# Hybrid encoder layer on one core: own PSUM banks for the up rows of even and odd tiles, earlier down additions, and silu as a sigmoid on ScalarE with a multiply on GpSimd during the attention

## What is computed

```python
h = x @ w_in                      # columns for three mixers
pool_out = multiscale_pool(h[..., :COL_Z], pool_w) * pool_scale
ssd_out = ssd_mixer(z, xbc, dt)   # silu(causal conv of width 4), chunked scan, gate silu(z), RMS norm
sb_out = stick_breaking_attention(q, k, v)      # 6 heads of 64, strictly causal, 128-query blocks
x = layer_norm(ALPHA * x + concat(pool_out, ssd_out, sb_out) @ w_out, ln1_g, ln1_b)
up = causal_depthwise_conv(x @ w_up, conv_w, conv_b)      # width 3, 2 x 2816 columns
ffn = (silu(up[..., :D_FF]) * up[..., D_FF:]) @ w_down
ple = sigmoid(x @ ple_w_gate) * (p @ ple_w_proj)
x = layer_norm(ALPHA * x + ffn + ple, ln2_g, ln2_b)
```

## Time and profile before

| | us |
|---|---|
| median of 3 runs | 1437.26 |
| lowest, highest | 1435.45, 1437.79 |
| the profiled execution | 1435.54 |
| its span in the trace | 1433.8 |

### The profile page before, as it was taken

One profiled execution on the slowest core, in us unless ns is written; L12 is line 12 of the kernel. 1 busy time (PEld: TensorE's weight loads), 2 busy tenths in 40 slices (PEclk: granted clock), 3 DMA queues, 4 the chain that ended last, 5 costly groups with the idle time before them and its releaser, 6 DMA issues.

```text
span 1433.8 us, 16333 instructions
## 1 busy us (share of the span) xinstructions
PE 1320.9 (92%) x6084; PEld 1057.1 (74%) x6084; DVE 879.5 (61%) x1060; ACT 507.4 (35%) x747; POOL 208.1 (15%) x141
## 2 busy tenths in 40 slices
PE   7999999899767999999999999999999999999993
PEld 5787788677655788788877777777777777777772
DVE  3536646534387845532467676767676776767778
ACT  4445445444544224312333232423232332323412
POOL 0000000000271000510012111111122021111116
PEclk9999999899988999999999999999999999999996
DMA  5101000000001311310020111102010101111102
GB/s 217 52 23 45 30 30 30 30 30 15 1 1 59 103 44 60 102 45 30 30 74 30 60 44 44 59 31 83 32 59 29 59 29 59 44 45 59 59 16 117
DMA packets 22947, 71.93 MB, mean 50 GB/s; under 512 B 2544, under 2 KB 2800, under 8 KB 22896
## 3 DMA queue, kind: packets, MB, share of 16 engines
q1 hardware_dynamic: 22896, 71.22, 14.6%
HBM read 67.02 MB, written 4.19 MB: 50 GB/s over the span
## 4 chain that ended last, share of the span: by engine, by line
PE 59%; DVE 18%; ACT 5%; issue 5%; DMA 1%; ACTq 1%; POOL 1%; DVEq 0%; SPq 0%; POOLq 0%
PE ps L667 12%; PE ps L669 12%; PE ps L668 12%; PE ps L1009 5%; PE ps L1011 5%; PE ps L1010 5%; DVE conv_ff L1764 4%; DVE conv_ff L1767 2%; PE ps L761 2%; ACT conv_ff L1343 2%; DVE w_lo L553 1%; PE ps L721 1%; PE ps L745 1%; PE ps L804 1%; ACT w_hi L548 1%
## 5 line engine op out<-in xcount | busy, mean ns | idle before, releaser
L1816 DVE TENSOR_TENSOR acc<-acc,ps 128x512 f32<-128x512 f32 x176 | 117.6, 685 | 71.2 <-PE ps L669 71.2
L667 PE MATMUL ps<-x_hi,w_hi 128*128 128x512 f32 x336 | 142.0, 423 | 14.1 <-DVE x_lo L502 10.5
L667 PE MATMUL ps<-h_hi,w_hi 128*128 128x512 f32 x320 | 127.6, 399 | 11.3 <-DVE acc L1816 11.3
L668 PE MATMUL ps<-x_lo,w_hi 128*128 128x512 f32 x336 | 134.6, 400 | 0.0
L669 PE MATMUL ps<-x_hi,w_lo 128*128 128x512 f32 x336 | 134.2, 399 | 0.0
L669 PE MATMUL ps<-h_hi,w_lo 128*128 128x512 f32 x320 | 126.6, 396 | 0.0
L668 PE MATMUL ps<-h_lo,w_hi 128*128 128x512 f32 x320 | 126.6, 396 | 0.0
L1009 PE MATMUL ps<-mix_hi,w_hi 128*128 128x512 f32 x320 | 126.6, 396 | 0.0
L1010 PE MATMUL ps<-mix_lo,w_hi 128*128 128x512 f32 x320 | 126.6, 396 | 0.0
L1011 PE MATMUL ps<-mix_hi,w_lo 128*128 128x512 f32 x320 | 126.6, 396 | 0.0
L1009 PE MATMUL ps<-t_hi,w_hi 128*128 128x512 f32 x240 | 96.8, 403 | 18.2 <-DVE conv_ff L1767 18.2
(11 more groups left out here) (240 smaller groups left out, 2847.9 us busy)
## 6 DMA issues: line engine op xcount, KB each, us to landing
raw<-u_up SPq DMA_DIRECT2D x44, 512.0 KB, 3.3
raw<-u_in SPq DMA_DIRECT2D x22, 512.0 KB, 3.3
down_raw<-u_down SPq DMA_DIRECT2D x44, 256.0 KB, 2.8
x_stage<-u_x SPq DMA_DIRECT2D x8, 512.0 KB, 7.7
raw<-u_out SPq DMA_DIRECT2D x8, 512.0 KB, 3.2
x_nat<-x_nat SPq DMA_DIRECT2D x8, 512.0 KB, 3.3
raw<-u_gate SPq DMA_DIRECT2D x8, 512.0 KB, 3.3
out<-o_norm SPq DMA_DIRECT2D x8, 512.0 KB, 2.6
```

The costliest lines, as they stand in the source:

```text
L667: mm(dst, w_hi, x_hi, start=first, stop=False)
L668: mm(dst, w_hi, x_lo, start=False, stop=False)
L1816: v.tensor_tensor(dst, dst, ps[:, bank, :], ALU.add).then_inc(dn_added, 1)
```

## The change

It has three parts.

1. In the feed-forward Y becomes banks 0, 1 for even pairs and 6, 7 for odd ones. The waits of PE follow: S2 of the even pair waits for the value row of the even pair before (`row_done` + 2 instead of + 4), S2 of the odd pair has no wait of its own except in the last chunk, and the first down product waits for all rows of the chunk before, where the third waited for three of them. In the last chunk the down products use banks 4, 5, 0, 1, and the final transposes pairs 1 and 3 instead of 0 and 1.
2. In DVE's order of a chunk the taps of the even gate row and the first five down additions come ahead of the split of A11 of the odd pair.
3. The ten silus become a sigmoid (ACT) and a multiply (GpSimd) at ticks of the attention: for the seven conv tiles at `GATE_AT`, the tick after the last tap (ticks 23, 29, 36, 53, 59, 66 and 73), for z0 to z2 at ticks 75, 77 and 80. Conv j waits for multiply j - 1 instead of for conv j - 1, at the earliest three ticks after the last tap: conv 6 moves from tick 66 to tick 68 and its taps from 68, 69, 70 to 69, 70, 72. The exp/ln table is loaded right after the barrier.

```diff
...
+GATE_LAG = 3
 CONV_AT, TAPS_AT = [], []
 for _name in H_TILES[:7]:
-    CONV_AT.append(max([evacuated_at(("tile", _name)) + 1] + [t[-1] + 1 for t in TAPS_AT[-1:]]))
+    CONV_AT.append(max([evacuated_at(("tile", _name)) + 1] + [t[-1] + GATE_LAG for t in TAPS_AT[-1:]]))
     TAPS_AT.append([s for s in range(CONV_AT[-1] + 1, NTICK) if s not in SPLIT_AT][:CONV - 1])
+GATE_AT = [t[-1] + 1 for t in TAPS_AT]
+for _name in H_TILES[7:10]:
+    GATE_AT.append(max(evacuated_at(("tile", _name)) + 1, GATE_AT[-1] + 2))
 DT_AT = evacuated_at(("turn", 3)) + 1
 SUMS_AT = 2 + next(s for s, d in enumerate(DONE_AT) if any(it[0] == "sums" for it in d))
...
             + [(d, k) for k in range(2) for d in (D0A, D1A, D0B, D1B)])
 PRODUCTS = {A11: 1, S1: 2, S2: 3, S3: 4, A12: 5, S4: 6, A22: 7}
 LASTC = CHUNKS - 1
-X_BANK, Y_BANK = (4, 2), 0
-DOWN_BANKS = (6, 7, 2, 3)
+X_BANK, Y_BANK = (4, 2), (0, 6)
+DOWN_BANKS, LAST_BANKS = (6, 7, 2, 3), (4, 5, 0, 1)
 def ops(c):
...
     dt_v = sem("dt_v")
     dt_a = sem("dt_a")
-    tap_done, conv_done, silu_done = sem("tap_done"), sem("conv_done"), sem("silu_done")
+    tap_done, conv_done, gate_done, silu_done = sem("tap_done"), sem("conv_done"), sem("gate_done"), sem("silu_done")
     d_full = sem("d_full")
     d_free = [sem("d_free%d" % i) for i in range(4)]
     decay_done = sem("decay_done")
...
     def up_row(pp, r):
-        b = Y_BANK if r else X_BANK[pp]
+        b = (Y_BANK if r else X_BANK)[pp]
         return ps[:, b:b + 2, :].rearrange("p b n -> p (b n)")
     def per_head(row, c):
...
             elif t == 2:
                 eng.wait_ge(u_free, 2 * KT)
             elif t == 3:
-                eng.wait_ge(row_done, 2)
                 column_tile(dst, slot, n, (1,)).then_inc(n1_read, 1)
             column_tile(dst, slot, n, (0,) if t == 3 else (0, 1)).then_inc(u_full, 1)
         def product(c, o, pp, it=0):
             first, second = slice(0, HALF), slice(HALF, S)
-            x, y = X_BANK[pp], Y_BANK
+            x, y = X_BANK[pp], Y_BANK[pp]
             bank, t_h, t_l = {
                 A11: (x, mh[:, 0:4, first], ml[:, 0:4, first]), S1: (x + 1, t1h, t1l), S2: (y + 1, t2h, t2l),
                 S3: (y, mh[:, 0:4, second], ml[:, 0:4, second]), A12: (x, mh[:, 4:8, first], ml[:, 4:8, first]),
...
             first = 16 * (c - 1 + pp)
             if k >= 4 or pp:
                 eng.wait_ge(dn_added, first + k - 3 + 16 * it)
-            bank = 4 + k % 4 if c == LASTC else DOWN_BANKS[k % 4]
+            bank = (LAST_BANKS if c == LASTC else DOWN_BANKS)[k % 4]
             h_h, h_l = (h2h, h2l) if pp else (hh, hl)
             for i in range(2):
                 o = ((D0A, D1A), (D0B, D1B))[j // 4][i]
...
             eng.wait_ge(row_done, 4 * (c - 1) + 1 + 4 * it)
             product(c, A11, 0, it)
             product(c, S1, 0, it)
-            eng.wait_ge(row_done, 4 * (c - 1) + 4 + 4 * it)
+            eng.wait_ge(row_done, 4 * (c - 1) + 2 + 4 * it)
             if c == 1:
                 eng.wait_ge(t_lo, 12)
             product(c, S2, 0, it)
...
             if c < LASTC:
                 eng.wait_ge(dn_added, 16 * (c - 1) + 16 + 16 * it)
             product(c, S1, 1, it)
-            eng.wait_ge(row_done, 4 * c + 2 + 4 * it)
+            if c == LASTC:
+                eng.wait_ge(row_done, 4 * (c - 1) + 4)
             product(c, S2, 1, it)
             product(c, S3, 1, it)
             eng.wait_ge(p1_done, 2 * (c - 1) + 2 + 2 * it)
...
             even(c, it)
             for k in range(16):
-                if k == 2:
-                    eng.wait_ge(row_done, 4 * (c - 1) + 3 + 4 * it)
+                if k == 0:
+                    eng.wait_ge(row_done, 4 * (c - 1) + 4 + 4 * it)
                 down(c, k, 0, it)
             even_last(c, it)
             odd(c, it)
...
             elif m >= 2:
                 eng.wait_ge(o_nrm, m - 1)
             for kt in range(KT):
-                last = turn(two(m % 2)[:, kt * P:(kt + 1) * P], acc[:, kt, m * P:(m + 1) * P])
+                last = turn(two((1, 3)[m % 2])[:, kt * P:(kt + 1) * P], acc[:, kt, m * P:(m + 1) * P])
             last.then_inc(o_full, 1)
         for t in range(4):
...
         even(LASTC)
         even_last(LASTC)
         odd(LASTC)
-        eng.wait_ge(row_done, 4 * LASTC + 1)
+        eng.wait_ge(row_done, 4 * LASTC + 2)
         for k in range(16):
             down(LASTC, k, 0)
         for k in range(16):
...
                 for hh_ in range(2):
                     wait_evacuated(eng, PLACE[(H_TILES[j], hh_)])
                 if j:
-                    eng.wait_ge(conv_done, j)
+                    eng.wait_ge(silu_done, j)
                 act(cv[:, j, :], ht[:, j, :], ACT.Identity, scale=param("conv_w", 4 * j + 3),
                     bias=param("conv_b", j)).then_inc(tap_done, 1)
+            if n in GATE_AT:
+                j = GATE_AT.index(n)
+                if j < 7:
+                    eng.wait_ge(conv_done, j + 1)
+                    act(ht[:, j, :], cv[:, j, :], ACT.Sigmoid).then_inc(gate_done, 1)
+                else:
+                    for hh_ in range(2):
+                        wait_evacuated(eng, PLACE[(H_TILES[j], hh_)])
+                    eng.wait_ge(silu_done, j)
+                    act(ht[:, 6, :], ht[:, j, :], ACT.Sigmoid).then_inc(gate_done, 1)
             if n == DT_AT + 1:
                 eng.wait_ge(dt_v, 1)
                 act(sm[:, 2, :], sm[:, 1, :], ACT.Exp).then_inc(dt_a, 1)
...
                 eng.wait_ge(decay_done, 1)
                 act(sm[:, 8, :], sm[:, 8, :], ACT.Exp).then_inc(dt_a, 1)
                 act(sm[:, 9, :], sm[:, 7, :], ACT.Exp).then_inc(dt_a, 1)
-            if n == NTICK + LAG - 1:
-                eng.wait_ge(conv_done, 7)
-                for j in range(3):
-                    act(cv[:, j, :], cv[:, j, :], ACT.Silu).then_inc(silu_done, 1)
         meet(eng, 1)
...
             pair = task_place(name)[0]
             return two(pair), d_free[pair]
-        for j in (3, 4):
-            act(cv[:, j, :], cv[:, j, :], ACT.Silu).then_inc(silu_done, 1)
+        nc.scalar.preload_act_table_set("natural_log_exp_and_others")
         for g in range(2):
             src, free = task("bt%d" % g)
             act(bn[:, g, :, :].rearrange("p m n -> p (m n)"), src, ACT.Copy).then_inc(free, 1)
-        for j in (5, 6):
-            act(cv[:, j, :], cv[:, j, :], ACT.Silu).then_inc(silu_done, 1)
-        for j in range(3):
-            act(ht[:, 7 + j, :], ht[:, 7 + j, :], ACT.Silu).then_inc(silu_done, 1)
         for g in range(2):
             src, free = task("cb%d" % g)
             act(cb[:, g, :], src, ACT.Copy).then_inc(free, 1)
...
             eng.wait_ge(hg_done, i + 1)
             act(cv[:, 3 + i, :], cv[:, i, :], ACT.Square).then_inc(sq_done, 1)
-        nc.scalar.preload_act_table_set("natural_log_exp_and_others")
         def pool_mean(i):
             eng.wait_ge(pool_sum, i + 1)
...
             eng.wait_ge(o_aff, m + 1)
             if m >= 4:
                 eng.wait_ge(stored[m % 4], 16 * (m // 4))
-            act(on[:, m % 4, :], two(m % 2), ACT.Identity, scale=st[:, m, 13:14],
+            act(on[:, m % 4, :], two((1, 3)[m % 2]), ACT.Identity, scale=st[:, m, 13:14],
                 bias=st[:, m, 12:13]).then_inc(o_nrm, 1)
...
         def combine(c, pp, step, it=0):
             n = 10 * (c - 1) + 5 * pp
-            x, y = X_BANK[pp], Y_BANK
+            x, y = X_BANK[pp], Y_BANK[pp]
             p1, u2 = pu[:, 0, :], pu[:, 1, :]
             product = {1: S2, 2: S1, 3: S3, 4: S4, 5: A22}[step]
             eng.wait_ge(prod_full, product_count(c, product, pp) + 14 * it)
...
                     eng.wait_ge(u_free, 2 * KT)
                     if first:
                         eng.wait_ge(dn_added, first + 16 * it)
-                bank = 4 + k % 4 if c == LASTC else DOWN_BANKS[k % 4]
+                bank = (LAST_BANKS if c == LASTC else DOWN_BANKS)[k % 4]
                 v.tensor_tensor(dst, dst, ps[:, bank, :], ALU.add).then_inc(dn_added, 1)
         eng.wait_ge(t_hi, 8)
...
             op_lo(c, D1B, 0, it)
             op_lo(c, A22, 0, it)
             combine(c, 0, 4, it)
+            taps(c, 0, 0, it)
+            add_down(c, 0, range(5), it)
             op_lo(c, A11, 1, it)
-            taps(c, 0, 0, it)
-            add_down(c, 0, range(8), it)
+            add_down(c, 0, range(5, 8), it)
             op_lo(c, S1, 1, it)
             op_lo(c, S2, 1, it)
             add_down(c, 0, range(8, 16), it)
...
         for m in range(MT):
             eng.wait_ge(o_full, m + 1)
-            statistics(m, two(m % 2)).then_inc(o_eps, 1)
+            statistics(m, two((1, 3)[m % 2])).then_inc(o_eps, 1)
             if m < 4:
                 add_down(c, 1, ((9,), (10, 11), (12, 13), (14, 15))[m])
             if m - 1 in GAIN_ON_VECTOR:
...
             else:
                 ins.then_inc(done, 1)
+        for j in range(10):
+            eng.wait_ge(gate_done, j + 1)
```

(2 more changed lines are left out.)

## The result

The changed kernel takes 1395.34 us (median of 4 runs, 1394.61 to 1396.12) against 1436.36 for the kernel before, timed beside it (4 runs): a ratio of 0.9717, 95% interval 0.9700 to 0.9733. The forecast was 1402.0, range 1394 to 1412; the result lies just under the forecast's own range of 1396 to 1408, and nearest to the 1397 of rival 4. The profiled execution took 1395.35 us, its span 1393.6 against 1433.8, so 40.2 us are to be found in the trace. Its lines are numbered four higher (three for L1009 to L1011): L667 is now L671, L1009 L1012, L1767 L1771, L1794 L1798, L1816 L1820, L451 L455, L1187 L1191.

The account below looks back on a forecast made before the run. PE sets the end in feed-forward and attention, so removed PE idle time counts; the SSD stage is the exception. 23.3 + 9.2 + 4.3 - 1.2 - 0.2 = 35.4 us less, forecast 1402.0 us, range 1394 to 1412 (own range 1396 to 1408).

Parts of the forecast that it names:

- rival 4: SSD stage gives more than the barrier: GpSimd's and DVE's turns fall well, clock stays up; 4 to 6 us more, 1397; chance 0.12.
- (a): Feed-forward, Y banks: all 19 waits of S2's up products for the conv taps go, 23.3 us with restarts.
- margin at S4: Feed-forward, even half: S4 waits for the second combination, which was read to end with 1.3 us in hand.
- (b): Feed-forward, chunks 1 to 9: first down addition comes 1.02 us sooner after combination 4, 9.2 us; bounds 0 and 13.1.
- (c): Barrier after the attention: without a table load and three silus PE starts the next stage 4.3 us sooner.
- (d): Attention takes on ten sigmoids and multiplies: conv 6 ahead of three table loads costs 1.2 us, z2's gate 0.2.
- Rivals 2 and 3: 2: GpSimd multiplies hold DVE, 23.4 us at most, 1425, chance 0.06; 3: gates break PE's clock, all ten 1476, chance 0.02.
- sign of 0.95: A granted clock under 0.95 from 100 to 375 us would show rival 3 and make the forecast wrong.
- (e): SSD stage, same code: shifted GpSimd/DVE pattern and PE's clock after the barrier wait taken at 0; bounds +3 and -4.
- (f): The end: final transposes and last downs use other banks, the waits are the same ones, 0.

Follow-up runs that it names:

- the runs with fills: Useless TensorE matmuls ahead of the barrier: twenty or ten on the kernel before (1434.81, 1434.57 us), twenty on the changed kernel with four chained ACT copies (1401.76 us).
- a_delay: Changed kernel with four chained ScalarE copies of 128x1024 ahead of the barrier after the attention, putting idle time back: 1402.34 us, ratio 0.9772.
- b_order: Kernel before with the order part alone (taps and five down additions ahead of the split of A11): 1427.02 us, ratio 0.9947.
- b_pefill: Kernel before with twenty unused 128x512 matmuls on TensorE ahead of the barrier, during the silus: 1434.81 us, ratio 0.9999.
- b_pefill10: Kernel before with ten unused 128x512 matmuls on TensorE ahead of the barrier: 1434.57 us, ratio 0.9996.
- b_gates: Kernel before with the gate part alone (silu as sigmoid on ACT and multiply on GpSimd in the attention): 1428.64 us, ratio 0.9961.

## Why the prediction was right, and where it was off

- (a) Banks, 23.3 us: measured alone, 23.65. No wait took the place of the taps, as said. The margin at S4 was mis-sized: 0.67 us instead of 1.3. The step that failed is that the queue ahead of the second combination "hangs on the end of the previous A22" and moves with it. The combinations of the odd half don't move with PE: the split ahead of combination 4 hangs on GpSimd's sum (ACT at 835.26 waits 1.37 us for it), while PE comes 0.8 us sooner. That chain is read from the trace; the 0.67 us are measured.
- (b) First additions, 9.2: 7.5 by the medians, 8.8 by span, 8.0 of these behind the second mark with a dip of the clock that costs 1.5. The chain after the change, counterpart of the earlier trace rows (timelines of ACT and DVE):

```profile
857.41 1.21 ACT L1347 ACTIVATE conv_ff<-ps,params 128x1024 f32<-128x1024 f32 x1 [2.41 <-DVE ps L1803]
...
858.79 1.28 DVE L1768 SCALAR_TENSOR_TENSOR conv_ff<-ps,params,conv_ff 128x1023 f32<-128x1023 f32 x1 [1.70 <-ACT conv_ff L1347]
...
861.42 1.87 DVE L1820 TENSOR_TENSOR acc<-acc,ps 128x512 f32<-128x512 f32 x3
```

  DVE's taps start 0.17 behind the end of ACT's (forecast 0.14), the addition follows without the split between, and PE waits 0.20, where 0.44 less the restart of 0.27 was forecast. The chunk: 62.06, forecast 62.0.
- (c) Barrier, 4.3: from the evacuation's end to PE's start 4.40 us before and 0.09 after. No drain beside the loads shows either, at the barrier or at tick 68: each load there starts within 0.02 us of the end of the activation ahead. The Trainium skill ("ScalarE: Activation LUTs", section "What ACT_TABLE_LOAD costs") adds a drain of some 1.38 us to a switch; the measurement decides against it here.
- (d) Attention, +1.4: the wait behind the three loads grew from 0.82 to 1.94 us, 1.1 where 1.2 was forecast. z2's gate cost nothing that a wait shows. Rivals 2 and 3 didn't come: the granted clock from 100 to 375 us is 0.98 before and after, over the sign of 0.95. The 0.7 us between two traces is too small a figure. The old attention ends its last evacuation at 375.1 to 375.9 us in four kernels whose granted clock from 250 to 300 us is 0.90, and at 373.34 in the fifth, where it is 0.93. With the gates it ends at 376.4 to 377.7 in five kernels at 0.90, and at 375.1 and 375.3 in two at 0.93. Like with like, the gates cost 1.8 us in the mean; where the part beyond the wait lies is open.
- (e) SSD stage, taken at 0, measured -3.9 up to the second mark: the term that was mis-sized, at the very end of its own bound (-4). The step that failed is the choice of 0 between -4 and +3: the clock's return had been priced there and then none of it taken, and the runs with fills show 3.1 and 3.2 us of it up to the feed-forward. It was rival 4 (chance 0.12), by the clock so far as the fills show it; that turns between GpSimd and DVE had a part in it was not tested.
- (f) The end, 0: PE's waits for the additions and for `o_norm` there are the ones of before.

So the mechanisms of (a) to (d) and (f) held, and the time was 6.7 us under the forecast. Between the two traces 3.9 lie in (e), 0.7 in the attention (by the traces above an accident of this pair), 0.2 in the feed-forward, together 4.8. The rest, 1.9 us, is the starting point: the sum was made against a profiled execution of 1435.54 and then taken off a median of 1437.26, while the kernel before had medians of 1434.5 to 1436.4 beside the changed kernel and the later runs.

## What to carry to other kernels

Count a wait of the engine that sets the end at its idle number plus a restart (0.25 to 0.27 us here), and check the sum against the period of a loop. A wait removed in one half of a loop shortens what is in hand in the other: follow each queue back to the engine that doesn't move with the one you sped up. Ahead of a stage that opens with matmuls, take idle time out by taking work away; work put in merely to keep TensorE busy won nothing here.

## What the runs showed of the hardware that I had not expected

TensorE's clock behind an idle time: at full speed behind 0.72 and 2.71 us, at a mean of 0.74 over 9.8 us behind 5.04 and of 0.82 over 9.7 us behind 4.93 (`a_delay`). How far it falls doesn't follow from the length of the wait alone. Behind one and the same wait of 3.65 us its mean over 12 us is 0.74 or 0.75 in three kernels and 0.86 to 0.88 in eleven. The three are those with a filled barrier 190 us earlier, and also those in which the clock falls earliest within the wait; no run here tells the two apart. Behind a wait of 1.9 us in the last chunk it dips in `b_order`, `b_pefill` and `b_pefill10` (0.93 over 25 us) and not in the kernel before or `b_gates` (1.00). The same code differs by 2.4 us in its first 376 us between traces, and the fast one has the higher clock around 280 us (0.93 instead of 0.90 over 50 us). It differs by 2.3 us in the stage behind the barrier too, so neither a milestone nor a distance between two marks is safe from a single trace. And the loss of an early gain need show in no wait at all: the runs with fills lose theirs where matmuls run at half speed and PE counts as busy.
